# Scan: the turned keys scaled by the gate and the decay of the mLSTM state, on ScalarE in place of VectorE

## Chip, cores and metric

One core of one Trainium2 chip. The metric is the device time of one execution in microseconds (us), the median of three. Matmuls run on TensorE (PE, its weight loads PEld), elementwise work on VectorE (DVE), ScalarE (ACT) and GpSimd (POOL); SyncE (SP) issues most of the DMAs.

## What is computed

The reference is a backbone of two layers. Each layer mixes tokens in four groups of heads, of which two are recurrences that run over the sequence in both directions: a gated linear attention (GLA) and an mLSTM. Cut to the two updates of state:

```python
def step(s, inp):                       # GLA
    d, u = inp
    return d[..., None] * s + u, s
...
w_k = jnp.exp(w_end - m_chunk[..., None])
upd_c = jnp.einsum('bhnl,bhnld,bhnlv->bhndv', w_k, k, v)     # mLSTM
...
    a = jnp.exp(fl + m_st - m_new)
    g = jnp.exp(mc - m_new)
    c_new = a[..., None, None] * c_st + g[..., None, None] * uc
```

A projection stands before the mixers; an output projection and a feed-forward stage (dense in layer 0, a mixture of experts in layer 1) stand behind them.

## The kernel before

The work is a row of phases, one after the other, each a block that all engines enter. The change is in `phase_scan` (L944), which runs once a layer. The 1280 tokens are 10 tiles of 128; each tile is visited once forwards (d = 0) and once backwards (d = 1), which makes U = 20 units, and unit u takes direction u % 2. State and working buffers have two halves, one a direction. When a unit is the first of two to visit a tile (`fresh`), its outputs are written; in the second they are added. Of tiles 0 and 1 the second visits come at once, in units 2 and 3; the other second visits are units 12 to 19, and the rest (4 to 11, and 0, 1) are first visits.

The order on each engine is written out by hand, with semaphores between them. In unit u:

- TensorE runs `scores(u+1)`: it turns the GLA keys (L999) and the mLSTM keys (L1001) into PSUM bank TR, then computes the GLA scores (L1006) and the mLSTM scores (L1011). Then `outputs(u)`: GLA output from the state Sp and the weights sg (L1026, L1031), mLSTM output from the state Sm and the weights ex (L1028, L1036). Then `updates(u)`: the updates of both states from the turned keys kdt (L1044) and kw (L1047), into banks UG and UM.
- Vector runs `weights(u+1)`: the turned mLSTM keys, scaled by the gate, from PSUM into kw (L1141), the masked GLA scores into sg (L1144), and ex times the mLSTM scores (L1148). Then the outputs of unit u: tmp and num (L1157, L1159), the second visit's GLA sum (L1164), the denominator (L1166 to L1169), the output (L1172, or L1174 and L1175). Then the states: the GLA update dsg (L1180), the mLSTM update dsm (L1182, which signals v_up), the decay of Sm (L1184), Sg (L1187, which signals v_g), Sm plus dsm (L1189, which signals v_st).
- Scalar copies the GLA output of a first visit (L1087), computes the exponentials ex of unit u+2 (L1068), copies the turned GLA keys of unit u+2 to kdt (L1077), and scales Sg into Sp when v_g comes (L1095).
- GpSimd masks the queries (L1117, L1119) and the rows of maxima (L1123), up to two units ahead, paced by the mLSTM scores (L1011). SP loads the rows of maxima (L1106).

`step(...)` lets an engine wait for the end of its own instruction before its next one. The tail phase (`phase_mix_project`, L1287 its first load) comes behind the scan.

Of the kernel before, what the change touches and what calls it, by code (L numbers as in the profile page):

```python
# [18 lines left out]
ACT = mybir.ActivationFunctionType  # L19
ALU = mybir.AluOpType  # L20
AX = mybir.AxisListType

P = 128
# [9 lines left out]
NH, HD = 4, 64  # L33
# [159 lines left out]
def bc(ap, n):  # L193

    return ap.unsqueeze(2).to_broadcast([ap.shape[0], ap.shape[1], n])
# [748 lines left out]
def phase_scan(nc, io, S, l, FM, TM, M):  # L944

    U = 2 * NT
    with Phase(nc, f"scan{l}") as ph:
        kdt = ph.sb("kdt", [P, 2, P])
# [10 lines left out]
        Sm = ph.sb("Sm", [P, 2, 2, 130])  # L959
        pe_tr, pe_sg, pe_sm, pe_og, pe_om, pe_u = (ph.sem(n) for n in (  # L960
            "transposed", "gla_scores_done", "mlstm_scores_done", "gla_out_done", "mlstm_out_done", "updates_done"))
        a_kdt, a_ex, a_og, a_sp = (ph.sem(n) for n in ("kdt_ready", "ex_ready", "gla_out_kept", "scaled_state_ready"))
        g_q, g_mx = ph.sem("masked_q_ready"), ph.sem("max_rows_masked")
        RING = 4
        mxr = ph.sb("max_rows", [P, RING, NH, P])
        mld = [ph.sem(f"max_rows_loaded{s}") for s in range(RING)]
        qg = ph.sb("qg", [P, 2, NH, P])
        qm = ph.sb("qm", [P, 2, NH, P])
        v_init, v_kw, v_sg, v_w, v_og, v_om, v_up, v_g, v_st, ch = (ph.sem(n) for n in (
            "states_zero", "kw_ready", "gla_weights_ready", "mlstm_weights_ready", "gla_out_added", "mlstm_out_read",  # L970
            "updates_read", "gla_state_ready", "states_ready", "dve_step"))
        if l == 1:
            filled = ph.sem("gate_stored")
# [15 lines left out]
        with nc.Block() as block:  # L989

            @block.tensor
            def _(pe):

                def scores(u):
                    d, n, t = unit(u)
                    if u >= 1:
                        pe.wait_ge(a_kdt, u)
                        pe.wait_ge(v_kw, u)
                    nc.tensor.transpose(ps[:, TR, 2 * P:3 * P], kd[:, d, t], c("ident"))  # L999
                    for j in range(2):  # L1000
                        x = nc.tensor.transpose(ps[:, TR, j * P:(j + 1) * P], FM[:, mk[j], t], c("ident"))  # L1001
                    x.then_inc(pe_tr, 1)
                    pe.wait_ge(g_q, u + 1)
                    if u >= 1:
                        pe.wait_ge(v_sg, u)
                    nc.tensor.matmul(ps[:, SG, :], kd[:, d, t], qg[:, d, :, :].rearrange("p a b -> p (a b)"),  # L1006
                                     start=True, stop=True).then_inc(pe_sg, 1)
                    if u >= 1:
                        pe.wait_ge(v_w, u)
                    for j in range(2):  # L1010
                        x = nc.tensor.matmul(ps[:, SM, j * 256:(j + 1) * 256], FM[:, mk[j], t],  # L1011
                                             qm[:, d, 2 * j:2 * j + 2, :].rearrange("p a b -> p (a b)"), start=True, stop=True)
                    x.then_inc(pe_sm, 1)

                def outputs(u):
                    d, n, t = unit(u)
                    if u >= 1:
                        if fresh[u - 1]:
                            pe.wait_ge(a_og, sum(fresh[:u]))
                        else:  # L1020
                            pe.wait_ge(v_og, u - sum(fresh[:u]))
                        pe.wait_ge(v_om, u)
                    if u >= 2:
                        pe.wait_ge(a_sp, u - 1)
                        pe.wait_ge(v_st, u - 1)
                    nc.tensor.matmul(ps[:, OG, 0:256], qd[:, d, t], Sp[:, d, :], start=True, stop=False, skip_group_check=True)  # L1026
                    for j in range(2):
                        nc.tensor.matmul(ps[:, OC, j * 130:(j + 1) * 130], FM[:, mq[j], t], Sm[:, d, j, :], start=True, stop=True)  # L1028
                    pe.wait_ge(v_sg, u + 1)
                    for h in range(NH):  # L1030
                        x = nc.tensor.matmul(ps[:, OG, h * HD:(h + 1) * HD], sg[:, d, h, :], TM[:, n, h * HD:(h + 1) * HD],  # L1031
                                             start=False, stop=(h == NH - 1), skip_group_check=True)
                    x.then_inc(pe_og, 1)
                    pe.wait_ge(v_w, u + 1)
                    for h in range(NH):
                        x = nc.tensor.matmul(ps[:, OI, h * 65:(h + 1) * 65], ex[:, d, h, :], vx[:, n, h, :], start=True, stop=True)  # L1036
                    x.then_inc(pe_om, 1)

                def updates(u):
                    d, n, t = unit(u)  # L1040
                    if u >= 1:
                        pe.wait_ge(v_up, u)
                    pe.wait_ge(a_kdt, u + 1)
                    nc.tensor.matmul(ps[:, UG, 0:256], kdt[:, d, :], TM[:, n, 0:256], start=True, stop=True)  # L1044
                    pe.wait_ge(v_kw, u + 1)
                    for j in range(2):
                        x = nc.tensor.matmul(ps[:, UM, j * 130:(j + 1) * 130], kw[:, d, 2 * j:2 * j + 2, :].rearrange("p a b -> p (a b)"),  # L1047
                                             vx[:, n, 2 * j:2 * j + 2, :].rearrange("p a b -> p (a b)"), start=True, stop=True)
                    x.then_inc(pe_u, 1)

                scores(0)
                pe.wait_ge(v_init, 1)
                for u in range(U):
                    if u + 1 < U:
                        scores(u + 1)
                    outputs(u)
                    updates(u)

            @block.scalar
            def _(act):  # L1060

                def decays(u):
                    d, n, t = unit(u)
                    if u >= 2:
                        act.wait_ge(pe_om, u - 1)
                    act.wait_ge(g_mx, u + 1)
                    for h in range(NH):
                        x = nc.scalar.activation(ex[:, d, h, :], mxr[:, u % RING, h, :], ACT.Exp,  # L1068
                                                 bias=tg[:, n, 0, d, h:h + 1], scale=-1.0)
                    x.then_inc(a_ex, 1)  # L1070

                def keys(u):
                    d, n, t = unit(u)
                    if u >= 2:
                        act.wait_ge(pe_u, u - 1)
                    act.wait_ge(pe_tr, u + 1)
                    nc.scalar.copy(kdt[:, d, :], ps[:, TR, 2 * P:3 * P]).then_inc(a_kdt, 1)  # L1077

                keys(0)
                decays(0)  # L1080
                decays(1)
                keys(1)
                for u in range(U):
                    d, n, t = unit(u)
                    if fresh[u]:
                        act.wait_ge(pe_og, u + 1)
                        nc.scalar.copy(og[:, n, :], ps[:, OG, 0:256]).then_inc(a_og, 1)  # L1087
                    if u + 2 < U:
                        decays(u + 2)
                        keys(u + 2)  # L1090
                    if u + 2 < U:
                        act.wait_ge(v_g, u + 1)
                        nn = order(d, u // 2 + 1)
                        act.wait_ge(pe_og, u + 1)
                        nc.scalar.activation(Sp[:, d, :], Sg[:, d, :], ACT.Copy, scale=em[:, d, 0, nn:nn + 1]).then_inc(a_sp, 1)  # L1095
# [31 lines left out]
            def _(dve):  # L1127
# [7 lines left out]

                def weights(u):
                    d, n, t = unit(u)
                    dve.wait_ge(a_kdt, u + 1)
                    if u >= 2:
                        dve.wait_ge(pe_u, u - 1)  # L1140
                    nc.vector.tensor_tensor(kw[:, d, :, :], ps[:, TR, 0:2 * P].rearrange("p (h c) -> p h c", c=HD),  # L1141
                                            bc(tg[:, n, 3, d, :], HD), ALU.mult).then_inc(v_kw, 1)
                    dve.wait_ge(pe_sg, u + 1)
                    nc.vector.copy_predicated(sg[:, d, :, :], keep[d].bitcast(I32).unsqueeze(1).to_broadcast([P, NH, P]),  # L1144
                                              ps[:, SG, :].rearrange("p (h t) -> p h t", t=P)).then_inc(v_sg, 1)
# [5 lines left out]
                for u in range(U):  # L1151
# [26 lines left out]
                    if u >= 1:  # L1178
# [2 lines left out]
                                                   op0=ALU.mult, op1=ALU.mult)  # L1181
                    nc.vector.tensor_tensor(dsm[:, :, :], ps[:, UM, 0:260].rearrange("p (a b) -> p a b", b=130),  # L1182
                                            c("blockm").unsqueeze(1).to_broadcast([P, 2, 130]), ALU.mult).then_inc(v_up, 1)
                    step(nc.vector.tensor_tensor(Sm[:, d, :, :], Sm[:, d, :, :], bc(dcol[:, 2 * d:2 * d + 2, n], 130), ALU.mult))  # L1184
                    if u >= 2:
                        dve.wait_ge(a_sp, u - 1)
                    nc.vector.scalar_tensor_tensor(out=Sg[:, d, :], in0=Sg[:, d, :], scalar=em[:, d, 1, n:n + 1], in1=dsg[:, :],  # L1187
                                                   op0=ALU.mult, op1=ALU.add).then_inc(v_g, 1)
                    nc.vector.tensor_tensor(Sm[:, d, :, :], Sm[:, d, :, :], dsm[:, :, :], ALU.add).then_inc(v_st, 1)  # L1189
                dve.wait_ge(v_st, U)  # L1190

# [1460 lines left out]
```

## Time and profile before

| | us |
|---|---|
| median of 3 runs (5227.7 to 5229.94) | 5229.01 |
| the profiled execution | 5224.78 |
| its span, first to last instruction | 5223.1 |
| PE busy in the span | 4834.2 (93%) |
| DVE busy | 2889.9 (55%) |
| ACT busy | 2186.8 (42%) |
| POOL busy | 364.9 (7%) |

Busy times are sums over the instructions of an engine; matmuls overlap and their ends are modelled. Times of a timeline are counted from the start of the span.

### The profile page before, as it was taken

How to read it: one execution, taken by the hardware profiler on the slowest of the kernel's cores; microseconds unless marked ns; L12 is line 12 of the kernel's file. 1: busy time of each engine (PE TensorE's matmuls, PEld its weight loads, DVE VectorE, ACT ScalarE, POOL GpSimd, SP SyncE). 2: the span in 40 equal slices, each digit the busy share in tenths (PEclk: the TensorE clock that was granted, in tenths of full speed). 3: DMA queues.
4: the chain of work that ended last, by engine and by line, in shares of the span. 5: the costliest groups of instructions: out<-in, count | busy, mean ns of one | idle time of the engine just before them, and what ended most of it. 6: DMA issues, size and time to landing. Idle time of an engine off the chain costs nothing. (4 is left out here: it accounts for less than half of the span.)

```text
span 5223.1 us, 61645 instructions
## 1 busy us (share of the span) xinstructions
PE 4834.2 (93%) x23048; PEld 3962.5 (76%) x23049; DVE 2889.9 (55%) x2875; ACT 2186.8 (42%) x2290; POOL 364.9 (7%) x343
## 2 busy tenths in 40 slices
PE   6998779999999799787899999999999999999994
PEld 5876657888888677565788888888888888888883
DVE  4369732111143446775854559974795544467476
ACT  3343322111132333333643457763674443456364
POOL 1004210000000100331000000000000000000001
PEclk8998889999999899888999999999999999999996
DMA  5321354223165432124965569985896555568576
GB/s 203 112 83 49 142 202 130 95 84 109 65 228 179 144 120 76 55 81 166 349 226 191 197 228 378 381 314 180 307 377 250 186 202 189 202 237 325 193 286 244
DMA packets 274867, 1014.16 MB, mean 194 GB/s; under 512 B 32496, under 2 KB 117808, under 8 KB 190400
## 3 DMA queue, kind: packets, MB, share of 16 engines
q1 hardware_dynamic: 260304, 956.27, 50.6%
q0 software_dynamic: 10992, 40.90, 2.1%
q10 hardware_dynamic: 3456, 15.47, 0.8%
q8 instruction: 71, 1.16, 0.1%
q14 instruction: 44, 0.36, 0.0%
HBM read 959.26 MB, written 53.30 MB: 194 GB/s over the span
## 5 line engine op out<-in xcount | busy, mean ns | idle before, releaser
L2116 PE MATMUL ps<-moe_gate_up_hi,moe_xh 128*128 128x512 f32 x2464 | 962.4, 391 | 4.4 <-DVE moe_gate_up_lo L2292 4.4
L2116 PE MATMUL ps<-moe_gate_up_hi,moe_xl 128*128 128x512 f32 x2464 | 961.5, 390 | 0.0
L2292 DVE TENSOR_TENSOR moe_gate_up_lo<-moe_wst,moe_gate_up_hi 128x2048 fp32r<-128x2048 f32 x424 | 952.0, 2283 | 16.6 <-ACT moe_gate_up_hi L2199 16.6
L2116 PE MATMUL ps<-moe_gate_up_lo,moe_xh 128*128 128x512 f32 x2464 | 959.5, 389 | 0.0
L2199 ACT CAST moe_gate_up_hi<-moe_wst 128x2048 fp32r<-128x2048 f32 x424 | 791.5, 1923 | 10.6 <-issue 6.6
L2395 DVE TENSOR_TENSOR moe_down_lo<-moe_wst,moe_down_hi 128x2048 fp32r<-128x2048 f32 x210 | 480.0, 2289 | 159.3 <-ACT moe_down_hi L2237 158.6
L2401 DVE TENSOR_TENSOR norm<-moe_sil,ps 128x512 f32<-128x512 f32 x210 | 143.5, 683 | 745.0 <-ACT moe_sil L2243 745.0
L2116 PEld LDWEIGHTS ps<-moe_gate_up_hi,moe_xh 128*128 128x128 f32 x2464 | 463.2, 188 | 101.5 <-DVE moe_gate_up_lo L2292 6.3
L2243 ACT ACTIVATE moe_sil<-ps 128x512 f32<-128x512 f32 x210 | 125.5, 598 | 984.0 <-PE ps L2116 983.9
L2116 PEld LDWEIGHTS ps<-moe_gate_up_hi,moe_xl 128*128 128x128 f32 x2464 | 463.0, 188 | 96.6
L2116 PEld LDWEIGHTS ps<-moe_gate_up_lo,moe_xh 128*128 128x128 f32 x2464 | 463.2, 188 | 95.2
L2237 ACT CAST moe_down_hi<-moe_wst 128x2048 fp32r<-128x2048 f32 x210 | 403.6, 1922 | 72.9 <-PE ps L2136 72.9
L2136 PE MATMUL ps<-moe_down_hi,moe_ah 128*128 128x512 f32 x1232 | 400.0, 405 | 9.6 <-DVE moe_al L2406 9.6
L1629 PE MATMUL ps<-hh,up_wh 128*128 128x512 f32 (+1 forms) x1056 | 378.1, 358 | 25.6 <-DVE up_wl L1733 20.7
L2136 PE MATMUL ps<-moe_down_lo,moe_ah 128*128 128x512 f32 x1232 | 383.3, 392 | 0.0
L2136 PE MATMUL ps<-moe_down_hi,moe_al 128*128 128x512 f32 x1232 | 380.3, 390 | 0.0
L1629 PE MATMUL ps<-hl,up_wh 128*128 128x512 f32 (+1 forms) x1056 | 375.5, 356 | 0.0
L1629 PE MATMUL ps<-hh,up_wl 128*128 128x512 f32 (+1 forms) x1056 | 375.2, 355 | 0.0
L1769 DVE TENSOR_TENSOR up_a<-up_sil,ps 128x512 f32<-128x512 f32 (+1 forms) x60 | 35.9, 599 | 447.8 <-PE ps L1629 447.8
L577 DVE TENSOR_TENSOR proj_w_lo<-proj_w_raw,proj_w_hi 128x1024 fp32r<-128x1024 f32 x122 | 151.9, 1245 | 233.3 <-ACT proj_w_hi L489 232.3
L489 ACT CAST proj_w_hi<-proj_w_raw 128x1024 fp32r<-128x1024 f32 x122 | 127.8, 1048 | 353.7 <-PE ps L433 194.0
L2136 PEld LDWEIGHTS ps<-moe_down_hi,moe_al 128*128 128x128 f32 x1232 | 231.2, 188 | 52.4
(383 smaller groups left out, 7566.2 us busy)
## 6 DMA issues: line engine op xcount, KB each, us to landing
moe_wst<-in_moe_packed SPq DMA_DIRECT2D x634, 1024.0 KB, 6.8
proj_w_raw<-in_w_in_packed SPq DMA_DIRECT2D x122, 512.0 KB, 3.4
down_wst<-in_ffn_w_down SPq DMA_DIRECT2D x66, 512.0 KB, 3.5
up_x<-in_ada_packed SPq DMA_DIRECT2D x12, 2048.0 KB, 8.4
ys_d<-moe_y POOLq DMA_DIRECT2D x15, 1024.0 KB, 4.4
tail_ada_w<-in_ada_packed SPq DMA_DIRECT2D x7, 2048.0 KB, 9.3
a_d<-up_a ACTq DMA_DIRECT2D x22, 640.0 KB, 3.0
FM<-in_w_out_packed SPq DMA_DIRECT2D x27, 512.0 KB, 4.4
```

Source lines behind the costliest of these rows:

```text
L489: nc.scalar.copy(wh[:, p % 2, :], raw[:, p % RAW, :]).then_inc(w_hi, 1)
L577: nc.vector.tensor_tensor(wlo[:, p % 2, :], raw[:, p % RAW, :], wh[:, p % 2, :].bitcast(F32), ALU.subtract).then_inc(split, 1)
L1629: x = nc.tensor.matmul(ps[:, 2 * pair + kind, :n], w[:, s, kind, k, :], h[:, k, t0:t0 + n], start=(k == 0 and j == 0), stop=(k == KD - 1 a ...
L1769: nc.vector.tensor_tensor(a[:, s, t0:t0 + n], sil[:, g, :n], ps[:, 2 * g + 1, :n], ALU.mult).then_inc(used, 1)
L2116: x = nc.tensor.matmul(ps[:, 2 * (q % 2) + i, :], xx[:, k, t], w[:, q % 2, k, :], start=(k == 0 and j == 0), stop=(k == KD - 1 and j == 2))
L2136: x = nc.tensor.matmul(ps[:, Y0 + 2 * i + half, :], aa[:, q % 2, i, c, :], w[:, q % 2, c, half * 512:(half + 1) * 512], start=(q == 0 and ...
L2199: nc.scalar.copy(guh[:, q % 2, 4 * j:4 * j + 4, :], wst[:, slot(n), :].rearrange("p (k n) -> p k n", k=4)).then_inc(hi, 1)
L2237: nc.scalar.copy(dnh[:, q % 2, :, :], wst[:, slot(n), :].rearrange("p (k n) -> p k n", k=2)).then_inc(hi, 1)
L2243: nc.scalar.activation(sil[:, :, :], ps[:, 2 * (q % 2):2 * (q % 2) + 2, 0:W], ACT.Silu).then_inc(silu, 1)
L2292: nc.vector.tensor_tensor(gul[:, q % 2, k, :], wst[:, slot(n), :].rearrange("p (k n) -> p k n", k=4), guh[:, q % 2, k, :].bitcast(F32), AL ...
L2395: nc.vector.tensor_tensor(dnl[:, q % 2, :, :], wst[:, slot(n), :].rearrange("p (k n) -> p k n", k=2), dnh[:, q % 2, :, :].bitcast(F32), AL ...
L2401: nc.vector.tensor_tensor(a[:, q % 2, :, :, :].rearrange("p i c f -> p i (c f)"), sil[:, :, :], ps[:, 2 * (q % 2):2 * (q % 2) + 2, W:2 * W ...
```

## The change

Scalar's `keys(u)` now also scales the turned mLSTM keys into kw, one activation a head with the gate as its scale, and one semaphore (`a_k`) says that kdt and kw are both there. The decay of Sm moves from Vector to two activations on Scalar, ahead of the exponentials of unit u+2, behind a wait for TensorE's pe_og. Vector waits for v_up ahead of Sg, and for Scalar's new signal `a_dec` ahead of the sum of Sm and dsm.

```diff
--- before.py
+++ after.py
@@ -959,15 +959,16 @@
         Sm = ph.sb("Sm", [P, 2, 2, 130])
         pe_tr, pe_sg, pe_sm, pe_og, pe_om, pe_u = (ph.sem(n) for n in (
             "transposed", "gla_scores_done", "mlstm_scores_done", "gla_out_done", "mlstm_out_done", "updates_done"))
-        a_kdt, a_ex, a_og, a_sp = (ph.sem(n) for n in ("kdt_ready", "ex_ready", "gla_out_kept", "scaled_state_ready"))
+        a_k, a_ex, a_og, a_sp, a_dec = (ph.sem(n) for n in (
+            "keys_ready", "ex_ready", "gla_out_kept", "scaled_state_ready", "mlstm_state_decayed"))
         g_q, g_mx = ph.sem("masked_q_ready"), ph.sem("max_rows_masked")
         RING = 4
         mxr = ph.sb("max_rows", [P, RING, NH, P])
         mld = [ph.sem(f"max_rows_loaded{s}") for s in range(RING)]
         qg = ph.sb("qg", [P, 2, NH, P])
         qm = ph.sb("qm", [P, 2, NH, P])
-        v_init, v_kw, v_sg, v_w, v_og, v_om, v_up, v_g, v_st, ch = (ph.sem(n) for n in (
-            "states_zero", "kw_ready", "gla_weights_ready", "mlstm_weights_ready", "gla_out_added", "mlstm_out_read",
+        v_init, v_sg, v_w, v_og, v_om, v_up, v_g, v_st, ch = (ph.sem(n) for n in (
+            "states_zero", "gla_weights_ready", "mlstm_weights_ready", "gla_out_added", "mlstm_out_read",
             "updates_read", "gla_state_ready", "states_ready", "dve_step"))
         if l == 1:
             filled = ph.sem("gate_stored")
@@ -994,8 +995,7 @@
                 def scores(u):
                     d, n, t = unit(u)
                     if u >= 1:
-                        pe.wait_ge(a_kdt, u)
-                        pe.wait_ge(v_kw, u)
+                        pe.wait_ge(a_k, u)
                     nc.tensor.transpose(ps[:, TR, 2 * P:3 * P], kd[:, d, t], c("ident"))
                     for j in range(2):
                         x = nc.tensor.transpose(ps[:, TR, j * P:(j + 1) * P], FM[:, mk[j], t], c("ident"))
@@ -1040,9 +1040,8 @@
                     d, n, t = unit(u)
                     if u >= 1:
                         pe.wait_ge(v_up, u)
-                    pe.wait_ge(a_kdt, u + 1)
+                    pe.wait_ge(a_k, u + 1)
                     nc.tensor.matmul(ps[:, UG, 0:256], kdt[:, d, :], TM[:, n, 0:256], start=True, stop=True)
-                    pe.wait_ge(v_kw, u + 1)
                     for j in range(2):
                         x = nc.tensor.matmul(ps[:, UM, j * 130:(j + 1) * 130], kw[:, d, 2 * j:2 * j + 2, :].rearrange("p a b -> p (a b)"),
                                              vx[:, n, 2 * j:2 * j + 2, :].rearrange("p a b -> p (a b)"), start=True, stop=True)
@@ -1074,7 +1073,10 @@
                     if u >= 2:
                         act.wait_ge(pe_u, u - 1)
                     act.wait_ge(pe_tr, u + 1)
-                    nc.scalar.copy(kdt[:, d, :], ps[:, TR, 2 * P:3 * P]).then_inc(a_kdt, 1)
+                    nc.scalar.copy(kdt[:, d, :], ps[:, TR, 2 * P:3 * P])
+                    for h in range(NH):
+                        x = nc.scalar.activation(kw[:, d, h, :], ps[:, TR, h * HD:(h + 1) * HD], ACT.Copy, scale=tg[:, n, 3, d, h:h + 1])
+                    x.then_inc(a_k, 1)
 
                 keys(0)
                 decays(0)
@@ -1085,6 +1087,12 @@
                     if fresh[u]:
                         act.wait_ge(pe_og, u + 1)
                         nc.scalar.copy(og[:, n, :], ps[:, OG, 0:256]).then_inc(a_og, 1)
+                    if u == 0:
+                        act.wait_ge(v_init, 1)
+                    act.wait_ge(pe_og, u + 1)
+                    for j in range(2):
+                        x = nc.scalar.activation(Sm[:, d, j, :], Sm[:, d, j, :], ACT.Copy, scale=dcol[:, 2 * d + j, n:n + 1])
+                    x.then_inc(a_dec, 1)
                     if u + 2 < U:
                         decays(u + 2)
                         keys(u + 2)
@@ -1135,11 +1143,8 @@
 
                 def weights(u):
                     d, n, t = unit(u)
-                    dve.wait_ge(a_kdt, u + 1)
                     if u >= 2:
                         dve.wait_ge(pe_u, u - 1)
-                    nc.vector.tensor_tensor(kw[:, d, :, :], ps[:, TR, 0:2 * P].rearrange("p (h c) -> p h c", c=HD),
-                                            bc(tg[:, n, 3, d, :], HD), ALU.mult).then_inc(v_kw, 1)
                     dve.wait_ge(pe_sg, u + 1)
                     nc.vector.copy_predicated(sg[:, d, :, :], keep[d].bitcast(I32).unsqueeze(1).to_broadcast([P, NH, P]),
                                               ps[:, SG, :].rearrange("p (h t) -> p h t", t=P)).then_inc(v_sg, 1)
@@ -1181,11 +1186,12 @@
                                                    op0=ALU.mult, op1=ALU.mult)
                     nc.vector.tensor_tensor(dsm[:, :, :], ps[:, UM, 0:260].rearrange("p (a b) -> p a b", b=130),
                                             c("blockm").unsqueeze(1).to_broadcast([P, 2, 130]), ALU.mult).then_inc(v_up, 1)
-                    step(nc.vector.tensor_tensor(Sm[:, d, :, :], Sm[:, d, :, :], bc(dcol[:, 2 * d:2 * d + 2, n], 130), ALU.mult))
+                    dve.wait_ge(v_up, u + 1)
                     if u >= 2:
                         dve.wait_ge(a_sp, u - 1)
                     nc.vector.scalar_tensor_tensor(out=Sg[:, d, :], in0=Sg[:, d, :], scalar=em[:, d, 1, n:n + 1], in1=dsg[:, :],
                                                    op0=ALU.mult, op1=ALU.add).then_inc(v_g, 1)
+                    dve.wait_ge(a_dec, u + 1)
                     nc.vector.tensor_tensor(Sm[:, d, :, :], Sm[:, d, :, :], dsm[:, :, :], ALU.add).then_inc(v_st, 1)
                 dve.wait_ge(v_st, U)
```

## Rows read from the trace of the kernel before

**Rows 1.** Windows, both scans: length; busy PE, PEld, DVE, ACT, POOL; clock; DMA
```profile
434.00:580.00 146.00, 127.06 (x737) 104.53 (x737) 131.29 (x304) 39.11 (x128) 76.95 (x80) 0.92 0.13 37
2152.00:2305.00 153.00, 128.38 (x737) 105.09 (x737) 130.90 (x303) 39.30 (x127) 77.08 (x80) 0.90 0.13 35
```

**Rows 2.** Timeline of Vector, a first visit: start, duration in us, engine, line
```profile
512.08 0.41 DVE L1141 TENSOR_TENSOR scan_kw<-ps,tg 128x256 f32<-128x256 f32 x1
512.41 0.73 DVE L1144 COPY_PREDICATED scan_sg<-cst,ps 128x512 f32<-128x512 int32 x1
...
515.89 0.41 DVE L1182 TENSOR_TENSOR scan_dsm<-ps,cst 128x260 f32<-128x260 f32 x1
...
516.79 0.72 DVE L1187 SCALAR_TENSOR_TENSOR scan_Sg<-scan_Sg,em,scan_dsg 128x256 f32<-128x256 f32 x1
...
518.52 0.72 DVE L1144 COPY_PREDICATED scan_sg<-cst,ps 128x512 f32<-128x512 int32 x1
```

**Rows 3.** Timeline of TensorE in the same unit; in brackets the idle time before
```profile
512.08 0.61 PE L1047 MATMUL ps<-vx,scan_kw 128*128 128x130 f32 x4
...
512.64 0.30 PE L999 MATMUL ps<-cst,kd 128*128 128x128 f32 x1
...
513.26 0.30 PEld L1006 LDWEIGHTS ps<-scan_qg,kd 128*128 128x128 f32 x2 [0.34 <-issue]
```

**Rows 4.** Timeline of Vector and GpSimd in a second visit
```profile
527.53 1.04 POOL L1117 TENSOR_TENSOR scan_qg<-qd,cst 128x512 f32<-128x512 f32 x1 [2.03 <-PE ps L1011]
527.56 1.30 DVE L1174 TENSOR_TENSOR scan_tmp<-scan_num,scan_den 128x256 f32<-128x256 f32 x1
...
529.93 0.41 DVE L1182 TENSOR_TENSOR scan_dsm<-ps,cst 128x260 f32<-128x260 f32 x1
530.04 1.26 POOL L1123 TENSOR_TENSOR scan_max_rows<-scan_max_rows,cst 128x512 f32<-128x512 f32 x1
530.26 1.33 DVE L1184 TENSOR_TENSOR scan_Sm<-scan_Sm,dcol 128x260 f32<-128x260 f32 x1
...
531.63 0.49 DVE L1187 SCALAR_TENSOR_TENSOR scan_Sg<-scan_Sg,em,scan_dsg 128x256 f32<-128x256 f32 x1
...
532.71 0.72 DVE L1144 COPY_PREDICATED scan_sg<-cst,ps 128x512 f32<-128x512 int32 x1
```

**Rows 5.** Timeline, starts of L1144 where the length of a unit changes
```profile
475.79 0.73 DVE L1144 COPY_PREDICATED scan_sg<-cst,ps 128x512 f32<-128x512 int32 x1
...
524.63 0.72 DVE L1144 COPY_PREDICATED scan_sg<-cst,ps 128x512 f32<-128x512 int32 x1
...
548.86 0.72 DVE L1144 COPY_PREDICATED scan_sg<-cst,ps 128x512 f32<-128x512 int32 x1
```

**Rows 6.** Timeline of Vector in a second visit, GpSimd's work of the scan done
```profile
2287.57 0.72 DVE L1144 COPY_PREDICATED scan_sg<-cst,ps 128x512 f32<-128x512 int32 x1
...
2291.70 0.42 DVE L1182 TENSOR_TENSOR scan_dsm<-ps,cst 128x260 f32<-128x260 f32 x1
2292.04 0.42 DVE L1184 TENSOR_TENSOR scan_Sm<-scan_Sm,dcol 128x260 f32<-128x260 f32 x1
2292.49 0.49 DVE L1187 SCALAR_TENSOR_TENSOR scan_Sg<-scan_Sg,em,scan_dsg 128x256 f32<-128x256 f32 x1
...
2293.57 0.71 DVE L1144 COPY_PREDICATED scan_sg<-cst,ps 128x512 f32<-128x512 int32 x1
```

**Rows 7.** Scalar: groups (busy us, mean ns, idle before), and one row of timeline
```profile
L1068 ACT ACTIVATE scan_ex<-scan_max_rows,tg 128x128 f32<-128x128 f32 x80 | 25.5, 390 | 8.0 <-POOL scan_max_rows L1123 7.1 <-PE ps L1036 0.9
L1095 ACT ACTIVATE scan_Sp<-scan_Sg,em 128x256 f32<-128x256 f32 x18 | 9.1, 508 | 83.8 <-DVE scan_Sg L1187 83.8
...
425.42 0.21 ACT L836 COPY tg<-ps 128x64 f32<-128x64 f32 x1 [1.27 <-PE ps L779]
```

**Rows 8.** Timeline where the first scan ends and the next phase begins
```profile
579.95 0.42 DVE L1189 TENSOR_TENSOR scan_Sm<-scan_Sm,scan_dsm 128x260 f32<-128x260 f32 x1
580.86 0.35 SPq L1287 DMA_DIRECT2D tail_ng<-in_gla_norm_g  x1
```

## Prediction

> **What bounds the kernel now.** I first asked for the stretches of the two scans, one per layer [rows 1]. Each lasts about 150 us of a profiled span of 5223.1 us. In both, Vector is busy 86 to 90% of the time, TensorE 84 to 87%, GpSimd about half, and Scalar only 39 of 146 us: 2.0 us in each of the 20 units of a scan. So the change takes work from the fullest engine to the one with most room. A share is an average, though; the timeline of one unit decides.
>
> A "first" unit (its tile is written for the first time) goes as in [rows 2]. Vector has no idle time: from one L1144 to the next is 518.52 - 512.41 = 6.11 us. TensorE follows it. It stands 0.34 us ahead of L1006 [rows 3], where it needs the weights that L1144 writes, and L999 starts 0.56 us after L1047, just behind the end of kw (512.08 + 0.41). L1047's four matmuls take about 0.45 by themselves, so that wait is 0 to 0.1 us. Without both waits TensorE needs 6.11 - 0.34 - (0 to 0.1) = 5.67 to 5.77 us a unit at this clock. That is the floor under Vector.
>
> A "second" unit (the tile is added to) goes as in [rows 4] and takes 8.08 us, though Vector has only about 0.7 us more work there. The rest is a collision. L1174 wants to start at 527.56, as GpSimd's L1117 has just started at 527.53, and takes 1.30 us. The decay L1184 starts at 530.26 inside GpSimd's L1123 and takes 1.33 us, up to 0.29 us after L1123 ends (531.30). After GpSimd has done its last unit, the same decay takes 0.42 and the unit 2293.57 - 2287.57 = 6.00 us [rows 6]. So Vector instructions with two inputs in SBUF wait out a running GpSimd instruction.
>
> The starts of L1144 give the classes [rows 5]: scan 0 has eight units of 6.11 (475.79 to 524.63), then three of 8.08 (up to 548.86). With those that the same timeline shows around them, and in scan 1, I count 18 of 6.1, 9 of 8.1, 3 of 7.1 to 7.4 and 4 of 6.0 us; the few left are the head.
>
> What is saved is kept: the last Vector instruction of the scan starts at 579.95 and the next phase's first load is issued at 580.86 [rows 8]. No transfer of the tail starts before, so nothing else fixes the end.
>
> **The change part by part.** *kw leaves Vector.* L1141 to L1144 is 0.33 us [rows 2], and Vector loses that in every unit. *The decay leaves Vector.* In the free unit, L1182 to L1187 is 2292.49 - 2291.70 = 0.79 us. What remains is L1182 with a new wait for its own end, since L1187 reads the GLA update. An instruction with such a step costs 2292.49 - 2292.04 = 0.45. Saved: 0.34 us free, and 516.79 - 515.89 - 0.45 = 0.45 us in the first unit. Vector then needs 6.00 - 0.67 = 5.33 us in a free second unit and 6.11 - 0.78 = 5.33 in a first unit: under TensorE's 5.67 to 5.77. So TensorE becomes the bound there, and the gain of a first unit is 0.34 to 0.44 us; I take 0.40, since kw's wait is likely real.
>
> *Scalar takes six small activations a unit*: four of 64 columns from PSUM, two of 130 in SBUF, with a scale from memory. No row has the first form. The nearest are the plain copy of 64 columns, 0.21 us, and the exponential of 128, 0.39 [rows 7]; at worst L1095's 0.51. That adds 4 x 0.21 + 2 x 0.39 = 1.6 up to 6 x 0.51 = 3.1 us; I take 2.0, since neighbours overlap. Scalar goes from 2.0 to 4.0 (at most 5.1) of a unit of 5.7, out of its 83.8 us of idle time in front of L1095. The Trainium skill (ScalarE: Activation LUTs, What ACT_TABLE_LOAD costs) gives 280 ns + 0.833 ns a column for an activation with one operand from memory: 333 ns for 64 columns, and 387 for 128, which agrees with the 390 here; the sum would be the same. *Where Scalar's new waits stand.* The decay waits for pe_og; the exponentials and keys behind it waited for the later pe_om anyway, so only the decay's own 0.7 us moves them. The keys of unit u+2 are turned at the start of TensorE's round u+1 and are first wanted a whole round (5.7 us) later: cover enough for 1 to 2 us. The decay is wanted by L1189, which stands behind L1187, 4.38 us after L1144 in [rows 2], and behind all that Vector does once pe_om has come, which is later than pe_og. Cost on the path: 0. If that cover were gone it would cost up to 1.5 us a unit. The PSUM bank of the turned keys is also freed by Scalar now, again a round ahead.
>
> *GpSimd, SP and DMA* are not touched. GpSimd's three steps are paced by TensorE's L1011, with two rounds of room.
>
> *The long units.* L1182 starts at 529.93; L1187 is now ready 0.45 later, at 530.38, in the decay's place, and has two SBUF inputs as well. So the collision stays and hits L1187: it ends some 0.35 after L1123, at 531.65. Before, L1187 started at 531.63 and the next L1144 came 1.08 later, 0.33 of it kw. Counting back its free 0.48 from 531.65 gives a start of 531.17, plus 0.75 is 531.92, in place of 532.71: 0.79 us saved. L1174 against L1117 stays as it is, because both hang on the same L1148. Bounds: 0 (another hold takes the gap) and 8.08 - 5.77 = 2.3 us (no collision left). I take 0.79, the value from the collision's own rows.
>
> **Sum.** 18 x 0.40 = 7.2; 9 x 0.79 = 7.1; 3 x 0.5 = 1.5 (half collisions); 4 x 0.3 = 1.2 (6.00 down to 5.7); and in the last two units of a scan TensorE has no more scores to make, so Vector sets the pace and its 0.67 counts in full: up to 1.3 a scan, of which I take 1.0: 2.0. Together 19.0 us. The profiled execution took 5224.8 us (1.7 around its span), 4.2 below the median of the runs shown, 5229.0; against the median I expect 5210. The profiled run itself would come to 5206.
>
> **Rivals.**
> *The collisions dissolve.* With TensorE as the bound, Vector no longer trails, and GpSimd's steps fall elsewhere in Vector's round. For it: in the first unit, same GpSimd work, the holds cost little. Against: a Vector total over 5.7 makes it trail again, and within two units the old phase is back. The time: 18 x 0.40 + 9 x 2.3 + 3 x 1.4 + 1.2 + 2.0 = 35.3 saved at full effect, 5194; part of it is likelier.
> *The holds only move.* L1187 or L1189 then waits out what the decay waited out, and the long units stay 8.1. The time: 18 x 0.34 + 1.2 + 1.0 = 8.3 saved, 5220.7.
> *Slower: first units are caught too.* All Vector steps now meet GpSimd at other moments. If L1187 meets a whole L1117 (1.04) and the read of num, L1166, a whole L1123 (1.26), a first unit takes 5.33 + 1.04 + 1.26 = 7.63 us: 18 x 1.52 = 27.4 lost, about 3 gained elsewhere, 5253. It decides from 0.34 us of added holds on (gain shrinks) and turns at 0.78 (slower). Against: Vector at 5.33 leaves L1187 beside L1117's end only, and L1123 ends before L1166. The Trainium skill (SBUF: State Buffer, Who interferes with whom) has the pair of ports that Vector and GpSimd share held by whoever starts first, for the whole instruction, "Issue order, not op shape, decides who blocks"; by that, a shift of 0.03 us like that of L1174 can be worth a microsecond, either way. The rows of the long unit agree.
> *It does nothing.* TensorE's own rate is the bound already and its 0.34 is only a record's artefact: 5229.
>
> **Chances.** Forecast (5205 to 5216) 0.57; dissolved, wholly or in part (5194 to 5204) 0.20; holds move (5221) 0.12; slower 0.07; nothing 0.04. A measurement of this kernel tells about 0.2%, 10.5 us, from no change. So faster by more is 0.57 + 0.20 and a little of the third, 0.78; within it 0.15; slower 0.07. The range is 5196 to 5220: the forecast, most of the dissolved case and the edge of the third, with 1 or 2 us for the places where TensorE's clock drops to 1.2 GHz moving.
>
> **What the changed profile would show.** Right: first units of 5.7 us, in which it is Vector that waits for TensorE; no more 0.34 ahead of L1006; long units near 7.3 with L1187 at about 1.2 us beside L1123; Scalar near 80 us busy in each scan and never the releaser of a long wait. Wrong: first units still at 6.1 or with a stretched L1166; waits of TensorE or Vector on Scalar's kw or decay; long units of 8.1, or 6; a scan shorter by under 5 or over 15 us.

## The result, and the profile after

The changed kernel takes 5187.35 us (5183.95 to 5189.56), the kernel before, run beside it, 5229.48: a ratio of 0.9919, 95% interval 0.9902 to 0.9936, 42 us less. The forecast was 5210, 19 us less, in a range from 5196 to 5220. The direction was right, the size was not: more than twice what was forecast.

The two scans first, as in [rows 1]. Columns: length; busy time of PE, PEld, DVE, ACT, POOL; granted clock; DMA share and GB/s.

```profile
434.00:560.00 126.00, 115.49 (x737) 99.62 (x737) 112.66 (x263) 68.39 (x246) 74.92 (x80) 0.96 0.15 42
2131.00:2265.00 134.00, 116.96 (x737) 100.20 (x737) 112.72 (x263) 68.62 (x247) 74.96 (x80) 0.94 0.15 40
```

Vector lost 18.6 us of busy time in the first scan (131.3 to 112.7), and the scan lost 20. Scalar went from 39 to 68 us, GpSimd kept its 75 to 77. TensorE is now busy 92% of the first scan. The next phase's first load, at 580.86 in [rows 8], is now here:

```profile
560.12 0.35 SPq L1293 DMA_DIRECT2D tail_ng<-in_gla_norm_g  x1
```

From the scan's first load (432.86 before, 432.39 after) to that row, the first scan takes 127.73 in place of 148.00 us; the second, counted from its first DMA of all (a store into `g_d`, which only layer 1 has), 136.02 in place of 154.87. That is 39.1 of the 40.8 us between the two profiled executions (5224.78 and 5183.95).

The rows that answer to [rows 2, 3], a first visit on Vector, GpSimd and TensorE. Lines moved by a few: L1144 is L1149, L1157 L1162, L1174 and L1175 are L1179 and L1180, L1187 L1192, L1189 L1195, L1117 L1125, L1119 L1127, L1123 L1131.

```profile
496.59 0.73 DVE L1149 COPY_PREDICATED scan_sg<-cst,ps 128x512 f32<-128x512 int32 x1
...
497.44 0.61 PE L1046 MATMUL ps<-vx,scan_kw 128*128 128x130 f32 x4
...
497.80 0.42 DVE L1162 TENSOR_TENSOR scan_tmp<-ps,tg 128x260 f32<-128x260 f32 x1
497.89 0.27 PE L999 MATMUL ps<-cst,kd 128*128 128x128 f32 x1
...
498.11 0.30 PEld L1006 LDWEIGHTS ps<-scan_qg,kd 128*128 128x128 f32 x2
...
500.19 1.04 POOL L1125 TENSOR_TENSOR scan_qg<-qd,cst 128x512 f32<-128x512 f32 x1 [1.82 <-PE ps L1011]
...
500.51 1.00 DVE L1192 SCALAR_TENSOR_TENSOR scan_Sg<-scan_Sg,em,scan_dsg 128x256 f32<-128x256 f32 x1
...
501.43 0.83 DVE L1195 TENSOR_TENSOR scan_Sm<-scan_Sm,scan_dsm 128x260 f32<-128x260 f32 x1
...
502.19 0.73 DVE L1149 COPY_PREDICATED scan_sg<-cst,ps 128x512 f32<-128x512 int32 x1
```

The unit takes 502.19 - 496.59 = 5.60 us. L1006 has no idle time before it any more, and L999 stands 0.45 behind L1046 instead of 0.56: in such a visit the profile shows TensorE waiting for nothing that Vector writes. Vector has no idle time either; its L1192 takes 1.00 us and its L1195 0.83, while GpSimd runs beside them.

New is GpSimd's place. It starts 500.19 - 497.80 = 2.39 us behind Vector's tmp. I call this the **offset**; before, it was 527.53 - 525.84 = 1.69 in the unit of [rows 4], and 1.69 to 1.71 in every unit from 1 to 14 of the first scan. The tmp of that unit, before:

```profile
525.84 0.41 DVE L1157 TENSOR_TENSOR scan_tmp<-ps,tg 128x260 f32<-128x260 f32 x1
```

What Scalar pays, in the groups of the first scan (busy us, mean ns, idle before):

```profile
L1078 ACT ACTIVATE scan_kw<-ps,tg 128x64 f32<-128x64 f32 x79 | 18.3, 319 | 0.0
L1094 ACT ACTIVATE scan_Sm<-scan_Sm,dcol 128x130 f32<-128x130 f32 x40 | 13.8, 393 | 3.6 <-PE ps L1031 3.6
L1103 ACT ACTIVATE scan_Sp<-scan_Sg,em 128x256 f32<-128x256 f32 x18 | 9.1, 508 | 41.0 <-DVE scan_Sg L1192 41.0
```

The small activations take 319 and 393 ns. The wait ahead of L1103 fell from 83.8 to 41.0 us: Scalar still has room.

**Unit by unit.** From the starts of tmp (L1157, L1162), first scan, in us (the columns behind "after" belong to the experiments):

```
unit             before  after  kw_only  decay_only  sum_late  tmp_early
0                  7.34   6.24     7.00        8.54      6.24       5.66
1                  6.11   5.60     5.78        5.42      5.60       5.59
2, 3 (second)      8.07   5.75     7.74   7.51/7.55  6.35/7.21 5.62/5.63
4                  6.12   5.28     5.78        5.42      5.09       5.54
5                  6.10   5.60     5.77        5.42      5.42       5.59
6 to 11            6.10   5.60     5.78        5.60      5.60       5.60
12, 13 (second)    8.08   5.75     7.74   7.57/7.54  6.35/7.23      5.62
14, 15 (second) 8.07/7.09 7.27/7.22 7.75  7.54/7.56      7.22 5.62/5.64
16, 17 (second)    5.99   5.33 5.96/5.68  5.65/5.67      5.08 5.42/5.60
18                 6.70   4.18     4.46        5.09      4.18       4.66
0 to 18, sum     128.43 108.63   121.56      120.07    111.86     105.40
```

More than half of what the forecast missed stands in units 2, 3, 12 and 13: 8.1 us became 5.75, where 7.3 was expected. Only 14 and 15 come out as long as forecast. The rest of this document is on why. When a Vector instruction with two inputs in SBUF starts while a GpSimd instruction runs and takes longer for it, I call it caught, or hit.

Unit 0 is no measure of the change: in profiles of the changed kernel and of kw_twice it takes 5.60, 6.24 or 8.21 us.

### The profile page after: what moved, and what is told of

The parts are those of the page before. It is cut to its first block and busy times, and to the rows that moved or that the text cites. A ratio compares the mean times of both kernels' runs of the same rounds, so it can differ in the third digit from the quotient of the medians.

```text
span 5182.3 us, 61771 instructions
## 1 busy us (share of the span) xinstructions
PE 4810.3 (93%) x23048; PEld 3953.1 (76%) x23049; DVE 2853.5 (55%) x2795; ACT 2246.0 (43%) x2530; POOL 360.8 (7%) x343
## 3 DMA queue, kind: packets, MB, share of 16 engines
q8 instruction: 71, 1.16, 0.1%
```

## The experiments

**Each part alone.** `kw_only` takes the changed kernel and gives the decay back to Vector; `decay_only` takes the kernel before and moves only the decay.

Of kw_only, against the changed kernel:

```diff
...
-                    act.wait_ge(pe_og, u + 1)
-                    for j in range(2):
-                        x = nc.scalar.activation(Sm[:, d, j, :], ...)
-                    x.then_inc(a_dec, 1)
...
-                    dve.wait_ge(v_up, u + 1)
+                    step(nc.vector.tensor_tensor(Sm[:, d, :, :], Sm[:, d, :, :], bc(dcol[:, 2 * d:2 * d + 2, n], 130), ALU.mult))
```

> Only the scaled keys move to ScalarE; the decay stays on VectorE. Theory A (room): what counts is whether Vector's own round fits under TensorE's 5.60 us. With kw alone it does not (6.11 - 0.33 = 5.78 in a first visit), so TensorE goes on waiting for Vector, Vector trails, and the long second visits stay: first visits 5.78, long ones 7.7, in all 10 to 15 us faster than before. Theory B (each part pays for itself): the gains of the two parts add up to the 42 us of the whole change; kw alone about 14 to 20, with long second visits of about 7.7.

> Only the decay of the mLSTM state moves to ScalarE; kw stays on VectorE. Theory A (room): Vector's first visit comes to 6.11 - 0.45 = 5.66 us, still over TensorE's 5.60 and with kw's wait in TensorE's way; long second visits at 7.6 remain: 14 to 20 us faster than before, and kw_only plus decay_only together fall short of 42. Theory B (each part pays for itself): the decay is the instruction that was caught by GpSimd's masks, so it brings 22 to 28 us, and the two sum to 42.

Measured: 5214.97 us (ratio 0.9978, 0.9968 to 0.9987) and 5214.04 (0.997, 0.9957 to 0.9982), beside 5229.21 before. That is 14 and 15 us, 29 together, not 42: the parts don't add up. kw_only's 14 alone could not tell the theories apart; decay_only's 15 and the sum do. One number of theory A was off: with the decay alone first visits already come down to TensorE's 5.60, not 5.66. Yet all second visits with GpSimd at work stay at 7.5, and 12 shows how they get there (decay_only; L1163 is tmp, L1180 the product, L1181 the sum with what is stored, L1196 Sm plus dsm):

```profile
522.88 0.41 DVE L1163 TENSOR_TENSOR scan_tmp<-ps,tg 128x260 f32<-128x260 f32 x1
...
524.93 1.04 POOL L1123 TENSOR_TENSOR scan_qg<-qd,cst 128x512 f32<-128x512 f32 x1 [1.82 <-PE ps L1011]
525.05 1.19 DVE L1181 TENSOR_TENSOR TM<-TM,scan_tmp 128x256 f32<-128x256 f32 x1
...
527.25 1.44 POOL L1129 TENSOR_TENSOR scan_max_rows<-scan_max_rows,cst 128x512 f32<-128x512 f32 x1
527.49 1.49 DVE L1196 TENSOR_TENSOR scan_Sm<-scan_Sm,scan_dsm 128x260 f32<-128x260 f32 x1
...
530.45 0.41 DVE L1163 TENSOR_TENSOR scan_tmp<-ps,tg 128x260 f32<-128x260 f32 x1
```

The offset is 524.93 - 522.88 = 2.05. Vector's sum wants to start 2.17 behind tmp (525.05), finds GpSimd 0.12 us ahead of it and takes 1.19 in place of 0.42; the next hit, 1.49, follows from the first. After this Vector trails, TensorE waits for it again, and the offset is 1.70 in the units that follow. Compare the changed kernel in unit 13, offset 522.57 - 520.34 = 2.23, where the sum comes first and it is GpSimd that waits (1.28 in place of 1.04), and unit 14, offset 2.08, where the sum is caught (here L1162 is tmp, L1180 the sum):

```profile
520.34 0.42 DVE L1162 TENSOR_TENSOR scan_tmp<-ps,tg 128x260 f32<-128x260 f32 x1
...
522.52 0.42 DVE L1180 TENSOR_TENSOR TM<-TM,scan_tmp 128x256 f32<-128x256 f32 x1
522.57 1.28 POOL L1125 TENSOR_TENSOR scan_qg<-qd,cst 128x512 f32<-128x512 f32 x1 [1.66 <-PE ps L1011]
...
526.09 0.42 DVE L1162 TENSOR_TENSOR scan_tmp<-ps,tg 128x260 f32<-128x260 f32 x1
...
528.17 1.04 POOL L1125 TENSOR_TENSOR scan_qg<-qd,cst 128x512 f32<-128x512 f32 x1 [1.50 <-PE ps L1011]
528.27 1.21 DVE L1180 TENSOR_TENSOR TM<-TM,scan_tmp 128x256 f32<-128x256 f32 x1
```

So a 5.75 us visit is 0.15 longer than TensorE's round, the offset slides by that (2.38, 2.23, 2.08), and the **edge** is near 2.17 us, where Vector's sum stands: with an offset above it the sum runs first, below it GpSimd does.

**Is Scalar covered?** `kw_twice` scales the keys twice.

```diff
+                    if u >= 2:
+                        act.wait_ge(a_k, u - 1)
+                    for h in range(NH):
+                        nc.scalar.activation(kx[:, d, h, :], ps[:, TR, h * HD:(h + 1) * HD], ACT.Copy, scale=tg[:, n, 3, d, h:h + 1])
                     for h in range(NH):
                         x = nc.scalar.activation(kw[:, d, h, :], ...)
```

> As the changed kernel, but ScalarE computes the scaled keys twice, the first time into a spare tile that nobody reads: 0.7 to 0.9 us more of ScalarE in each unit, ahead of the keys' signal. If ScalarE is covered by a whole round of TensorE, as the prediction said: same time as the changed kernel within 2 us, units still 5.60 and 5.75. Rival, that ScalarE now sets the pace of the 5.75 us second visits or of the units that still collide: 0.15 us or more for each of 12 such units, up to 0.7 us for each of all 38, 5 to 27 us slower.

Scalar's busy time in the first scan rose from 68.4 to 84.8 us, 0.8 a unit. Measured 5186.89 us against the changed kernel's 5187.35, and the units of the first scan are the changed kernel's within 0.02 us. So Scalar still has 0.8 us a unit to spare, and what the change gave it costs nothing.

**Less Vector time, more hits.** `sum_late` was meant to stop the slide and beat the changed kernel.

```diff
+                    dve.wait_ge(ch, step.n)
...
-                        step(nc.vector.tensor_tensor(tmp[:, :, 0:HD], num[:, :, 0:HD], bc(den[:, :], HD), ALU.mult))
-                        nc.vector.tensor_tensor(on, on, tmp[:, :, 0:HD], ALU.add)
+                        nc.vector.tensor_tensor(tmp[:, :, 0:HD], ...).then_inc(ch, 1)
+                        step.n += 1
...
+                    if not fresh[u]:
+                        dve.wait_ge(ch, step.n)
+                        nc.vector.tensor_tensor(on, on, tmp[:, :, 0:HD], ALU.add).then_inc(ch, 1)
+                        step.n += 1
```

> As the changed kernel, but in second visits Vector adds the output to the stored one behind the two state updates, so that two waits for its own last instruction (0.12 us each) are filled with work. Theory A (room): the 5.75 us second visits exceed TensorE's 5.60 by 0.15 each and Vector's lag grows until GpSimd's mask starts in front of Vector's product, which makes the last two long (7.27 and 7.22). With 0.24 less they all fit: 5.60 each, no unit of 7.2, about 8 us faster than the changed kernel. Rival (the collision is tied to the end of the scan, whatever the lag): the two units of 7.2 stay and only 12 x 0.15 = 2 us are gained.

Measured 5192.96 us (0.993, 0.9914 to 0.9947): 5.6 slower than the changed kernel. Free of GpSimd a second visit did get shorter (5.08 in place of 5.33), but beside it units 2 and 12 take 6.35. In the changed kernel the sum ran ahead of GpSimd; moved behind dsg and dsm it runs into L1125, here in unit 12, and is followed by two more instructions that GpSimd holds (0.83 us each):

```profile
521.35 1.04 POOL L1125 TENSOR_TENSOR scan_qg<-qd,cst 128x512 f32<-128x512 f32 x1 [1.81 <-PE ps L1011]
521.76 0.91 DVE L1192 TENSOR_TENSOR TM<-TM,scan_tmp 128x256 f32<-128x256 f32 x1
```

Theory A as I had put it, that only Vector's total counts, falls here. What counts as well is which two-input instruction stands where GpSimd is at work.

**Room without moving a two-input instruction back.** `tmp_early` fills Vector's wait between tmp and num with the product of ex and the scores; `both_fill` also lets Sg wait for dsg's own signal.

Of tmp_early (`weights2(u + 1)` is the product of ex and the scores of unit u + 1, and of nothing else; from unit 1 on it stands here, behind tmp):

```diff
-                    step(nc.vector.tensor_tensor(tmp[:, :, :], ...))
+                    nc.vector.tensor_tensor(tmp[:, :, :], ...).then_inc(ch, 1)
+                    step.n += 1
+                    if 1 <= u < U - 1:
+                        weights2(u + 1)
+                    dve.wait_ge(ch, step.n)
```

> Only the first of the two edits of both_fill: tmp ahead of ex times the scores, 0.11 us less of Vector a unit. Theory (offset): a second visit comes to 5.64, the slide is 0.04 a unit, the offset stays above the edge for all four units: 5 to 8 us faster than the changed kernel. Rival: v_w now comes 0.34 us later, TensorE waits ahead of L1011 again and all first visits get longer: 36 x up to 0.3 us, up to 10 us slower.

> The changed kernel with two of Vector's waits for itself filled: tmp is computed ahead of ex times the scores, and Sg waits for dsg's own signal instead of v_up; no instruction more or less, and no two-input instruction moved later. Theory (offset): a second visit costs Vector 5.75 against TensorE's 5.60, so GpSimd's start slides from 2.38 to 2.23 to 2.08 us behind Vector's tmp, and below about 2.2 the hits begin. With 0.1 to 0.2 us less per visit the slide stops and the two units of 7.2 us at the end of each scan go: 6 to 9 us faster than the changed kernel. Rival (the hits come whenever four second visits follow each other, or the time saved in Vector is taken back by the ports): within 2 us of the changed kernel, or slower as with sum_late.

Measured 5178.99 us (0.9901, 0.9885 to 0.9918) and 5182.54 (0.9907, 0.989 to 0.9923). In tmp_early every unit from 1 to 15 of the first scan takes 5.54 to 5.64; unit 14, where the changed kernel was caught (L1167 is tmp, L1188 the product, L1189 the sum):

```profile
527.34 0.41 DVE L1167 TENSOR_TENSOR scan_tmp<-ps,tg 128x260 f32<-128x260 f32 x1
...
529.53 0.42 DVE L1188 TENSOR_TENSOR scan_tmp<-scan_num,scan_den 128x256 f32<-128x256 f32 x1
529.99 0.43 DVE L1189 TENSOR_TENSOR TM<-TM,scan_tmp 128x256 f32<-128x256 f32 x1
530.26 1.06 POOL L1125 TENSOR_TENSOR scan_qg<-qd,cst 128x512 f32<-128x512 f32 x1 [1.75 <-PE ps L1011]
```

The sum stands 0.27 us ahead of GpSimd. With no such hit in units 14 and 15, units 0 to 18 take 3.2 us less in either scan (105.4 in place of 108.6), and those two units alone 3.2 less. Counted from the first load or store to the next phase, as in the result, the scans are 3.1 and 2.4 us shorter, 5.5 in all, where the two profiled executions are 4.9 apart (5183.95 and 5179.01) and the medians 8.4; the part of the 8.4 that lies outside the scans is not explained. The second edit, both_fill's, brings nothing more that these runs can tell: TensorE's 5.60 is the bound already. Run again beside the changed kernel:

> The changed kernel once more, so that the next one is compared with it under the same conditions: 5184 to 5190 us.

> The kernel of tmp_early once more. Theory (offset): the gain is in the scans, 3.1 us in the first and 2.4 in the second by the first profile, so 4 to 9 us under the changed kernel run beside it. Rival: the first profile's gain was chance, within 2 us of the changed kernel.

Measured 5188.6 us (0.9922, 0.9906 to 0.9939) and 5181.43 (0.9911, 0.9895 to 0.9928), 7.2 apart after 8.4 the first time. tmp_early is the fastest version of this study.

**TensorE the bound, and the edge.** `pe_short` leaves out one of the two products of Sm with the queries, from unit 2 on (half of the mLSTM's state output is not computed).

> The changed kernel with one of the two state products of the mLSTM output left out on TensorE (from unit 2 on), 0.22 us less of TensorE a unit; Vector, Scalar and GpSimd do the same instructions. If TensorE is the bound of first visits, they come to 5.38 us. Theory (offset): GpSimd's start then stands 2.16 us or less behind Vector's tmp, under the edge, so the second visits turn long (7.2 to 7.6) from the first or second on, and the kernel as a whole gets slower by 4 to 12 us although only work was taken out. Rival (Vector alone sets the pace): 5.60 and 5.75 stay. Rival (no edge): everything 0.2 faster, 8 us gained.

First visits 6 to 11 come to 5.37 us: TensorE set the 5.60. Vector's L1193 (the changed kernel's L1192) takes 0.78 us in them in place of 1.00, so the 0.22 that TensorE no longer needs came off Vector's held time. Vector, Scalar and GpSimd do the same instructions as in the changed kernel, but the offset is now 2.15, just under the edge, and unit 12 is caught at once (L1163 is tmp, L1126 GpSimd's mask, L1181 the sum):

```profile
519.57 0.41 DVE L1163 TENSOR_TENSOR scan_tmp<-ps,tg 128x260 f32<-128x260 f32 x1
...
521.72 1.04 POOL L1126 TENSOR_TENSOR scan_qg<-qd,cst 128x512 f32<-128x512 f32 x1 [1.59 <-PE ps L1011]
521.75 1.29 DVE L1181 TENSOR_TENSOR TM<-TM,scan_tmp 128x256 f32<-128x256 f32 x1
```

GpSimd is 0.03 us ahead, and units 12 to 15 take 7.34, 7.22, 7.22, 7.22. Units 0 to 18 take 116.15 us in place of 108.63 in the first scan and 110.86 in place of 108.62 in the second: less work, a longer scan. Not all of the first scan's 7.5 is the edge's. Units 0 and 1, ahead of the edit, give 1.5 (unit 0 takes 8.22), and unit 18 gives 2.1, for TensorE's granted clock was 0.50 there. Units 2 to 17 are 4.0 us longer in the first scan and 3.0 in the second. I don't compare its whole time (5089.76): its values differ, and layer 1 sends tokens to experts by them.

**Does GpSimd's instruction hold Vector's?** `mask_small_before` cuts L1123 of the kernel before to 4 columns (the mask of the maxima is not applied beyond them).

> The kernel before, with GpSimd's mask of the rows of maxima cut from 512 to 4 columns (the rest of the mask is left out). If L1184 is blocked by that instruction, it falls from 1.33 to about 0.42 us and the long second visits from 8.08 to about 7.2, while L1174 keeps its 1.30 beside the masked queries and first visits keep 6.11. Rival (Vector waits there for something else, a semaphore or a drain): 8.08 stays.

```profile
527.35 1.04 POOL L1117 TENSOR_TENSOR scan_qg<-qd,cst 128x512 f32<-128x512 f32 x1 [3.10 <-PE ps L1011]
527.38 1.29 DVE L1174 TENSOR_TENSOR scan_tmp<-scan_num,scan_den 128x256 f32<-128x256 f32 x1
...
529.86 0.19 POOL L1123 TENSOR_TENSOR scan_max_rows<-scan_max_rows,cst 128x4 f32<-128x4 f32 x1
530.08 0.41 DVE L1184 TENSOR_TENSOR scan_Sm<-scan_Sm,dcol 128x260 f32<-128x260 f32 x1
```

L1184 falls from 1.33 to 0.41 and the long visits from 8.07 to 7.15 to 7.17, while L1174 keeps its 1.29 and first visits their 6.10. So the hit on L1184 was GpSimd's L1123. The hit on L1174 this run leaves in place; that it is GpSimd's too rests on the kernel before, where the same instruction takes 0.43 us once GpSimd is done (second scan, unit 17), and on units 2, 12 and 13 of the changed kernel, where GpSimd starts behind the product and the product takes 0.42. Of the kernel before:

```profile
2290.51 0.43 DVE L1174 TENSOR_TENSOR scan_tmp<-scan_num,scan_den 128x256 f32<-128x256 f32 x1
```

(The whole time, 4986.39 us, is not compared, for the same reason.)

**The order alone.**

> The kernel before with nothing moved to ScalarE, only tmp computed ahead of ex times the scores. Theory (room): Vector's first visit is 6.11 - 0.11 = 6.00, TensorE still waits for Vector, GpSimd's start stays tied to Vector's product, and the long second visits stay long (about 8.0): 3 to 6 us under the kernel before, so the order alone does not do what the move does. Rival (the order alone shifts GpSimd's start past Vector's product, whatever the load): the 8.1 us visits go to about 6.0 and 15 us or more are gained.

Measured 5222.0 us (0.9985, 0.9975 to 0.9994), 7 under the kernel before. First visits 6.00, long ones mostly 7.73: tmp_early's order without the move to Scalar doesn't free the second visits. The move made the room, and the order uses it.

## Why the prediction was right in direction and wrong in size

*What bounds the scan: right.* Vector set the pace, TensorE was the floor under it, nothing else fixed the end. The floor was put at 5.67 to 5.77; it is 5.60. I had counted the waits ahead of L1006 and L999. A third stood ahead of L1011, which came 0.94 behind L1006 before and comes 0.86 behind it now. Before and after:

```profile
513.29 1.10 PE L1006 MATMUL ps<-scan_qg,kd 128*128 128x512 f32 x2
513.80 0.19 PEld L1011 LDWEIGHTS ps<-scan_qm,FM 128*128 128x128 f32 x1 [0.24 <-DVE scan_ex L1148]
...
514.23 1.03 PE L1011 MATMUL ps<-scan_qm,FM 128*128 128x256 f32 x4
```

```profile
498.22 1.02 PE L1006 MATMUL ps<-scan_qg,kd 128*128 128x512 f32 x2
498.65 0.19 PEld L1011 LDWEIGHTS ps<-scan_qm,FM 128*128 128x128 f32 x1 [0.24 <-issue]
...
499.08 1.03 PE L1011 MATMUL ps<-scan_qm,FM 128*128 128x256 f32 x4
```

One sign that was to go with this did not show: in first visits 4 to 11 Vector does not wait for TensorE. Vector's spare time is spent in GpSimd's holds (L1192 1.00 us, where it takes 0.48 in units 16 and 17; L1195 0.83 for 0.42), and GpSimd starts behind TensorE's L1011; that TensorE's pace reaches Vector by way of these holds is my reading, which pe_short's 0.78 supports.

*Scalar's new work costs nothing: right*, shown by kw_twice. It added 1.5 us a unit, where I took 2.0. The Trainium skill's formula (ScalarE: Activation LUTs, What ACT_TABLE_LOAD costs) gave an estimate of 333 ns for 64 columns, where 319 were measured.

*The terms of the sum*, from the unit lengths of both scans, forecast and measured: first visits 7.2 and 9.8; the nine visits of 8.1 us 7.1 and 17.9; the three of 7.1 to 7.4, 1.5 and 1.3; the four of 6.0, 1.2 and 2.7; head and end of the scans 2.0 and 7.4. Sum 19.0 and 39.1. Of the 20.1 us between the two sums, 10.8 are the nine visits of 8.1 us.

*The step that failed* is this one: "L1174 against L1117 stays as it is, because both hang on the same L1148." It held as long as TensorE's L1011 waited for L1148, as its row of before shows. The same text had just found that TensorE would wait for Vector no longer, so GpSimd, which starts behind L1011, is not tied to L1148 any more. The end of the output's matmuls (L1036, whose end is modelled) now stands 0.68 us ahead of tmp, where it stood 1.88, and GpSimd starts 2.38 instead of 1.69 behind tmp, past both the product and the sum. So the step counted 0.79 us for a visit of 8.1, and seven of the nine gave 2.3. The rival "the collisions dissolve" named this, and I gave it 0.20 on the ground that a Vector total above TensorE's round brings the old phase back within two units. It does, and the runs show it: after two second visits, in units 14 and 15. But with only two or four second visits in a row that have GpSimd beside them, four of a scan's six are over by then.

*Ends of the scans.* The 2.0 was an undersized term, and its reason missed the larger part. Unit 18 alone went from 6.70 to 4.18 in the first scan and from 5.75 to 4.18 in the second, 4.1 us, and this is TensorE's clock, not Vector's work. Before, TensorE stands still 2.08 us (second scan 2.09) ahead of the last unit's L1026, and then its matmuls run at a granted clock of 0.50, the level of 1.2 GHz: L1031 takes 1.81 us (1.76 in the second scan, where the clock falls there). Now it stands 1.17 (1.16), the clock stays at 1.00, 2.4 GHz, and L1031 takes 1.00. Before and after, L1026 and the window behind it (columns as in the result):

```profile
570.39 1.22 PE L1026 MATMUL ps<-scan_Sp,qd 128*128 128x256 f32 x2 [2.08 <-DVE FM L1164]
...
570.40:575.50 5.10, 5.10 (x22) 4.92 (x23) 3.09 (x10) 0.00 (x0) 0.00 (x0) 0.50 0.01 2
```

```profile
552.50 0.70 PE L1026 MATMUL ps<-scan_Sp,qd 128*128 128x256 f32 x2 [1.17 <-DVE FM L1169]
...
552.50:555.30 2.80, 2.80 (x23) 2.75 (x24) 2.63 (x9) 0.70 (x2) 0.00 (x0) 1.00 0.00 0
```

The prediction had the clock only as 1 or 2 us of its range, not in its sum. No run isolates it: in pe_short TensorE stands 1.61 us there in both scans, and the clock fell in the first and not in the second. Unit 0 gives 2.2 of the rest, and as said it varies by itself; the time behind the last tmp gives 0.3 a scan, the decay that is gone.

*The slower rival* (first visits caught) did not come. Vector's L1192 is stretched in each of them, 1.00 in place of 0.72, but inside the 5.60. The page behind it held: the Trainium skill (SBUF — State Buffer, Who interferes with whom) says that issue order decides who blocks, and the rows above show it to 0.03 us.

*Open.* 1.7 of the 40.8 us lie outside the scans; no run here says where they come from. The time of the changed kernel spreads over 6 us. One repeat was caught in unit 3 of the first scan (7.25 in place of 5.75), so part of that spread is the edge; that it is all of it was not shown.

## What to carry to other kernels

When work leaves the engine that sets the pace, ask what was tied to that pace: a third engine, whose instructions hold the first one's up, may start at another moment, and that can be worth more than the instructions moved. In a loop where two engines hold each other up, one visit is not enough for a forecast; follow the offset over several, since a round that is 0.15 us too long costs 0.15 in each of two units and 1.7 in the third. And before freeing time on Vector, look at which of its two-input instructions will stand beside GpSimd. Where TensorE stands still near the end of a loop, read the granted clock behind that wait: some of the time there may be the clock's and not the work's.

## What the runs showed that I had not expected

A lead of 0.03 to 0.12 us of GpSimd over a Vector instruction with two inputs in SBUF makes that instruction take 1.19 to 1.30 us in place of 0.42, and with the hit that follows, makes the second visit 7.2 to 7.6 us in place of 5.75. Taking 0.22 us of matmul time out of each unit made units 2 to 17 of the two scans 4.0 and 3.0 us longer (pe_short), and taking 0.25 us out of Vector's second visits made the kernel 5.6 us slower (sum_late). And 4.1 of the 39.1 us that the scans gained are the last unit of each, which no longer runs at half the granted clock.
